# A two-layer encoder step: the modulation product moved into the input projections in four column groups, and the squares of the norms added up on VectorE

## The chip, the core and the metric

The kernel runs on one core of one Trainium2 chip. TensorE multiplies matrices (a product is a weight load, LDWEIGHTS, and a MATMUL that streams columns past the loaded weights), VectorE (DVE), ScalarE (ACT) and GpSimd (POOL) work element by element, and SyncE (SP) issues most DMAs. Each engine runs its own instructions in order and waits for others by semaphores. The metric is the device time of one execution in microseconds (us); lower is better.

## The reference, cut to what matters

A trunk of two layers is applied to 512 prompt tokens and 32 sample tokens, D = 1024, everything in float32.

```python
def trunk_layer(x, c, past, lw, layer):
    mod = einsum('bd,de->be', silu(c), lw['ada_w']) + lw['ada_b']     # 1024 -> 6144, per group
    sh1, sc1, g1, sh2, sc2, g2 = split(mod, 6)
    h = rms_norm(x, lw['norm_mix_g']) * (1 + sc1) + sh1
    z = h @ lw['w_in']                                # 2250 columns for the mixers, 3072 for the gates
    ...                                               # sparse, forgetting and pooling mixers
    x = x + g1 * (merged @ lw['w_out'])
    h = rms_norm(x, lw['norm_ffn_g']) * (1 + sc2) + sh2
    f = swiglu(h, ...) if layer % 2 == 0 else moe_ffn(h, ...)
    return x + g2 * f
```

`mod` is the modulation: for each of the two groups (prompt and sample) one row of 6144 values from the group's conditioning `c`, by a weight matrix of 1024 x 6144 (24 MB) per layer.

## The kernel before, in words

Activations lie transposed: `xT` and `hT` hold 8 blocks (k = 0 to 7) of 128 features by 544 tokens. A program order written out by hand runs on each engine; a planner class (`Ring`) works out, for four weight buffers `slots` of 1 MB, how often each has been filled (`full`) and which product must have begun before SP may fill it again (`free`). Per layer the stages are:

1. **First norm.** ACT squares the 8 blocks of x (L1299). TensorE sums them over the features with a matrix of ones, 8 blocks by 2 halves (`norm_sums`, L788). DVE takes mean and epsilon (L1570), ACT the root (L1304), DVE the reciprocal with one Newton step and the products `x * r` (`stats`, L1572 to L1577).
2. **Modulation** (L817 to L827). A loop of 6 rounds with 4 buffers each: TensorE multiplies silu(c) (`csil`, 128 x 2 per k) by 256 columns of the weights, 8 blocks of k, into 2 partitions; ACT copies the 2 x 256 row out (L1344), TensorE turns it into columns with two small products (L825). When all 24 blocks are through, DVE adds the bias (L1584) and forms the gains `scl` (L1587).
3. **norm** (ACT, L1316) applies gain and shift to each k, ACT rounds the result into a high part `hH` (L1323), DVE takes the rest as low part `hL` (L1592).
4. **z projection** (L843). 9 column blocks of 250, 5 token tiles each, so 45 tiles; a tile is 8 k by 3 products (high times high, high times low, low times high). ACT splits off the high part of each weight block (`proj_high`, L1336, into `wz`), POOL the low part (L674). ACT copies each tile out (L1352). DVE rotates queries and keys once 20 tiles are there (`rope`, L1607 to L1612).
5. Indexer scores (L870), gate projection (L882), selection, pooling, attention (L1002 to L1052), branch and output projections (L798, L882), residual sums on DVE (L1781).
6. **Second norm**: the same as stage 1 on the new x (`squares`, `norm_sums`, `stats`, `norm`).
7. Layer 0: a SwiGLU in two halves (L1235) written as loops on PE, ACT and DVE. Layer 1: a loop over expert passes (L1186, L1214).

What sets the order around the change: TensorE meets the modulation between the norm sums and the z projection, and the residual sums of the SwiGLU's last half come just before the first norm of layer 1. SP's queue holds the fills of one stage after those of the stage before. ACT calls the first `proj_high` of the gate projection while the last z block is multiplied.

```python
for k in range(KD):
    pe.wait_ge(sq_ready, KD * n + k + 1)
    for h in range(2):
        last = mm(ps[:, h, 0:HALF], ones[:, :], sqs[n % 2][:, k, h * HALF:(h + 1) * HALF], ...)
```

Of the kernel before, what the change touches and what calls it, by code (L numbers as in the profile page):

```python
# [52 lines left out]
MBLK, MSLOT = 20, 10  # L53
GU = 12
# [138 lines left out]
def encoder_step(nc, t_in, t_out):  # L193
    ring = Ring()
    for L in range(DEPTH):
        ring.phase(("ada", L), 6, [1] * 4)
        ring.phase(("z", L), ZITER, [1] * ZBODY)
        ring.phase(("gates", L), GITER, [1] * GBODY, slots=2)
        ring.phase(("pooled", L), 1, [1])
        ring.ghost()  # L200
        ring.phase(("branch", L), 2, [2] * 2)
        ring.phase(("out", L), 2, [1] * 2, slots=2)
        ring.ghost()

        if L == 0:
            ring.phase(("ffn", L), HALVES, [2] * FB + [1] * KD, "split")

    ctx = ExitStack()
    with ctx:
# [20 lines left out]
        def sem(name):  # L230
            return ctx.enter_context(nc.semaphore(name))
# [18 lines left out]
        csil = sb("csil", [P, KD, 2])  # L250
        mod = sb("mod", [P, 48, 2])
        scl = sb("scl", [P, 2, KD, 2])
        negcum = sb("negcum", [BH, KEYS])
# [74 lines left out]
        mrow = oTf[0:2, 4 * NTOK:4 * NTOK + 1024].rearrange("p (j n) -> p j n", j=4)  # L328
# [84 lines left out]
        ada_row, ada_copied, ada_done = sem("ada_row"), sem("ada_copied"), sem("ada_done")  # L413
# [7 lines left out]
        csil_ready = sem("csil_ready")  # L421
        mod_ready = sem("mod_ready")
        sq_ready, ms_ready, v_ready, root_ready = sem("sq_ready"), sem("ms_ready"), sem("v_ready"), sem("root_ready")
# [69 lines left out]

        def moe_landed(n, b):

            return n * 32 + 16 * (b // MSLOT + 1)
# [11 lines left out]
        def _(sp):  # L508
# [13 lines left out]
            for L in range(DEPTH):  # L522
                ada = t_in["ada_w"][L].rearrange("(k p) n -> p k n", p=P)
# [4 lines left out]
                def ada_fill(it):  # L528
                    for j in range(4):
                        fill(("ada", L), it, j, [(cols(j, 256), ada[:, :, ds(it * 1024 + j * 256, 256)])])  # L530

                if L == 0:
                    ada_fill(0)
                with sp.Fori(1 if L == 0 else 0, 6) as it:
                    if L == 0:
                        for j in range(4):
                            sp.wait_ge(block_begun, it * 4 + (j - 2))
                            sp.dma_start(cols(j, 256), ada[:, :, ds(it * 1024 + j * 256, 256)]).then_inc(slot_full[j], 16)
                    else:
                        ada_fill(it)  # L540
                with sp.Fori(0, ZITER) as it:
                    for j in range(ZBODY):
                        fill(("z", L), it, j, [(cols(j, ZB), w_in[:, :, ds(it * (ZBODY * ZB) + j * ZB, ZB)])])
# [99 lines left out]
        def _(pool):  # L643
# [14 lines left out]
            for L in range(DEPTH):  # L658
# [6 lines left out]
                pool.dma_start(poolm, t_in["c_pool"]).then_inc(pool_mats_loaded, 16)  # L665
# [13 lines left out]
                low(("gates", L), 0, 0)  # L679

# [75 lines left out]
        def _(pe):  # L756
# [26 lines left out]
            def norm_sums(n, releases=False):  # L783

                for k in range(KD):
                    pe.wait_ge(sq_ready, KD * n + k + 1)
                    for h in range(2):
                        last = mm(ps[:, h, 0:HALF], ones[:, :], sqs[n % 2][:, k, h * HALF:(h + 1) * HALF],  # L788
                                  start=(k == 0), stop=(k == KD - 1))
                        if releases and k == h == 0:  # L790
                            last.then_inc(block_begun, 1)
                last.then_inc(ms_ready, 1)
# [11 lines left out]
            for L in range(DEPTH):  # L804
# [6 lines left out]
                pe.wait_ge(v_ready, 2 * L + 1)  # L811
                with pe.Fori(0, 6) as it:
                    for j in range(4):
                        landed(("ada", L), it, j)
                        w = slots[:, j, :].rearrange("p (k n) -> p k n", k=KD)
                        for k in range(KD):
                            last = mm(ps[0:2, j, 0:256], csil[:, k, :], w[:, k, :], start=(k == 0), stop=(k == KD - 1))  # L817
                            if k == 0:
                                last.then_inc(block_begun, 1)
                        last.then_inc(ada_row, 1)  # L820
                        for i in ([j - 1] if j else []) + ([3] if j == 3 else []):

                            pe.wait_ge(ada_copied, it * 4 + (24 * L + i + 1))
                            for f in range(2):
                                last = mm(ps[:, 7, ds(it * 16 + (i * 4 + f * 2), 2)], mrow[:, i, f * P:(f + 1) * P],  # L825
                                          ident[0:2, 0:2], start=True, stop=True)
                            last.then_inc(ada_done, 1)  # L827

                with pe.Fori(0, ZITER) as it:
                    for j in range(ZBODY):  # L830
                        wh, wl, _ = proj_parts(("z", L), j)
                        for t in range(TILES):
                            g = j * TILES + t
                            if g >= TILES - 1:

                                pe.wait_ge(z_evac, it * (ZBODY * TILES) + (NZ * L + g - TILES + 2))
# [11 lines left out]
                    pe.wait_ge(z_evac, it * (ZBODY * TILES) + (NZ * L + ZBODY * TILES - 1))  # L848
# [257 lines left out]
                if L == 1:  # L1106
# [21 lines left out]

                    for s in range(2):
                        last = nc.tensor.transpose(ps[0:KD, 4, s * P:(s + 1) * P], mod[:, M_G2:M_G2 + KD, s], ident[:, :])  # L1130
# [149 lines left out]
        def _(act):  # L1280
# [10 lines left out]
            A(csil[:, :, :], vecT[:, 0, V_C:V_C + 16].rearrange("p (s k) -> p k s", s=2), ACT.Silu).then_inc(csil_ready, 1)  # L1291

            def squares(n, x_there):
                for k in range(KD):
# [32 lines left out]
            for L in range(DEPTH):  # L1327
                def proj_high(name, it, j):
# [4 lines left out]
                    act.wait_ge(block_begun, ring.released(name, it, j, ZBODY if name[0] == "z" else 2))  # L1333
# [4 lines left out]
                squares(2 * L, xu(L - 1, "ffn") - KD if L else None)  # L1338
                root(2 * L)

                with act.Fori(0, 6) as it:
                    for j in range(4):
                        act.wait_ge(ada_row, it * 4 + (24 * L + j + 1))
                        A(mrow[:, j, :], ps[0:2, j, 0:256], ACT.Copy).then_inc(ada_copied, 1)  # L1344
                norm(2 * L, lambda k, s: scl[:, 0, k, s:s + 1],
                     lambda k, s: mod[:, M_SH1 + k, s:s + 1], L + 1, split=True)

                def z_blocks(it):
                    for j in range(ZBODY):
                        for t in range(TILES):  # L1350
# [3 lines left out]
                            if t == 0:  # L1354

                                if j + 1 < ZBODY:
                                    proj_high(("z", L), it, j + 1)
                                elif isinstance(it, int):
                                    proj_high(("gates", L), 0, 0)
                                else:  # L1360
                                    proj_high(("z", L), it + 1, 0)

                with act.Fori(0, ZITER - 1) as it:
                    z_blocks(it)
                z_blocks(ZITER - 1)
# [80 lines left out]
                for j in range(2):  # L1446
                    proj_high(("out", L), 1, j)
                squares(2 * L + 1, xu(L, "start"))
                root(2 * L + 1)
                norm(2 * L + 1, lambda k, s: scl[:, 1, k, s:s + 1],  # L1450
                     lambda k, s: mod[:, M_SH2 + k, s:s + 1], 0)
# [66 lines left out]
                with act.Fori(0, HALVES) as it:  # L1518
# [22 lines left out]
                    for j in range(FB + KD):  # L1541
# [3 lines left out]
                        high(j, 1)  # L1545

        @block.vector
        def _(dve):
            ch = Chain(dve, dve_chain)
            V = nc.vector  # L1550
            V.memset(ones[:, :], 1.0).then_inc(memsets, 1)
# [26 lines left out]

            for L in range(DEPTH):
                stats(2 * L)  # L1580

                dve.wait_ge(ada_done, 24 * (L + 1))
                bias = vecT[:, L, V_ADAB:V_ADAB + 48].unsqueeze(2).to_broadcast([P, 48, 2])
                ch.link(V.tensor_tensor(mod[:, :, :], ps[:, 7, 0:96].rearrange("p (b s) -> p b s", s=2), bias, ALU.add))  # L1584
                for i, (sc0, g0) in enumerate(((M_SC1, V_NMIX), (M_SC2, V_NFFN))):
                    gain = vecT[:, L, g0:g0 + KD].unsqueeze(2).to_broadcast([P, KD, 2])
                    last = V.scalar_tensor_tensor(scl[:, i], mod[:, sc0:sc0 + KD, :], 1.0, gain, ALU.add, ALU.mult)  # L1587
                last.then_inc(mod_ready, 1)
# [26 lines left out]

                dve.wait_ge(z_evac, NZ * L + 4 * TILES)
                rope(IQ, IH)
                rope(IK, 1)
                rope(AQ, AH + 1)

# [322 lines left out]
                with dve.Fori(0, HALVES) as it:  # L1943
# [3 lines left out]
                    ch.enter(it, 0, 2 * FB)  # L1947

# [16 lines left out]
                    for j in range(FB + KD):  # L1965
# [5 lines left out]
                        if d >= 0:  # L1971
                            dve.wait_ge(unit_done[1], it * nb + (n0 * nb + FB + d + 1))
                            dve.wait_ge(x_upd, it * KD + (xu(L, "out") + d))
                            residual((d + 2) % 4, d, M_G2)
                    dve.wait_ge(unit_done[1], it * nb + (n0 * nb + FB + KD))
                    dve.wait_ge(x_upd, it * KD + (xu(L, "out") + KD - 1))
                    residual((KD + 1) % 4, KD - 1, M_G2)
                ch.leave(HALVES)
# [56 lines left out]
```

## Time and profile before

| what | us |
|---|---|
| median of 3 runs | 2545.38 |
| lowest, highest | 2542.48, 2548.31 |
| profiled execution, own time | 2540.93 |
| its span | 2539.1 |
| TensorE busy in the span | 2376.3 |
| DVE, ACT, POOL busy | 761.7, 579.2, 300.5 |

The span is the time from the first to the last instruction of one profiled execution. A row of the chain of waits gives start, length and what ran; the chain is followed back from the last instruction, each step to what released it. A row of the timeline names start, length, engine, line, operation, target and source tile, their shapes, how many were merged (x) and, in brackets, how long the engine had been idle and who released it. "PEclk" is the share of TensorE's full clock that was granted.

### The profile page before, as it was taken

What the parts mean: (1) busy time and instruction counts of PE and PEld (TensorE: products, weight loads), DVE (VectorE), ACT (ScalarE), POOL (GpSimd) and SP (SyncE); (2) the same over time, 40 slices, a digit from 0 to 9 for tenths busy, and PEclk for the clock granted to TensorE, in tenths of its full rate; (3) what the DMA queues carried; (4) which work ended last, traced back from release to release, by engine and by line L of the source; (5) the groups of instructions that cost most, each with busy time, mean ns of one, the idle gap of its engine ahead of it and who ended that gap; (6) DMA issues with size and microseconds to landing.
All of it is one profiled execution on the core that took longest, in us unless ns stands there. A gap on an engine that the chain in (4) does not pass through costs nothing.

```text
span 2539.1 us, 40187 instructions
## 1 busy us (share of the span) xinstructions
PE 2376.3 (94%) x16529; PEld 2115.6 (83%) x16531; DVE 761.7 (30%) x1561; ACT 579.2 (23%) x1158; POOL 300.5 (12%) x194
## 2 busy tenths in 40 slices
PE   6989899899959999999989899899989999999995
PEld 3479799776859999996479799666869999999995
DVE  2013490453433333332013580453430000000014
ACT  2042422131142222211042422231241111111111
POOL 2023343000210000000023332000210000000001
PEclk9989999896979999999989999896999999999998
DMA  6722222230243223225721232000266888777883
GB/s 223 240 82 65 85 83 83 66 106 15 77 120 83 64 81 100 84 65 175 237 69 55 86 99 67 13 1 25 79 213 202 247 261 267 247 231 232 244 283 114
DMA packets 333972, 328.04 MB, mean 129 GB/s; under 512 B 7659, under 2 KB 325593, under 8 KB 333305
## 3 DMA queue, kind: packets, MB, share of 16 engines
q1 hardware_dynamic: 326720, 303.41, 38.9%
q0 software_dynamic: 5888, 18.52, 2.2%
q10 hardware_dynamic: 1256, 4.60, 0.5%
q8 instruction: 78, 1.28, 0.2%
q14 instruction: 30, 0.24, 0.0%
HBM read 310.29 MB, written 26.16 MB: 133 GB/s over the span
## 4 chain that ended last, share of the span: by engine, by line
PE 92%; ACT 3%; DVE 2%; issue 1%; POOL 1%; DMA 1%; DVEq 0%; POOLq 0%; ACTq 0%; SPq 0%
PE ps L1235 16%; PE ps L882 16%; PE ps L1186 15%; PE ps L843 10%; PE ps L1214 7%; PE ps L817 7%; PE ps L798 5%; PE ps L1040 4%; PE ps L1024 3%; PE ps L1002 2%; PE ps L788 1%; PE ps L825 1%; ACT hT L1316 1%; PE ps L947 1%; PE ps L1163 1%
## 5 line engine op out<-in xcount | busy, mean ns | idle before, releaser
L1235 PE MATMUL ps<-hR,wR 128*128 128x272 f32 x2112 | 270.3, 291 | 31.2 <-DVE wR L1953 26.6
L882 PE MATMUL ps<-hH,slotsR 128*128 128x272 f32 x1536 | 293.7, 291 | 3.7 <-ACT oT L1385 3.7
L1235 PEld LDWEIGHTS ps<-hR,wR 128*128 128x128 f32 x2112 | 269.8, 191 | 31.8 <-DVE wR L1953 27.0
L882 PEld LDWEIGHTS ps<-hH,slotsR 128*128 128x128 f32 x1536 | 244.0, 190 | 4.4 <-issue 4.4
L674 POOL TENSOR_TENSOR slotsR<-slots,slotsR 128x1024 fp32r<-128x1024 f32 x64 | 154.5, 2435 | 699.2 <-ACT slotsR L1336 699.2
L843 PE MATMUL ps<-wz,hH 128*128 128x250 f32 (+1 forms) x720 | 206.7, 287 | 21.4 <-POOL slotsR L674 15.0
L882 PE MATMUL ps<-hL,slotsR 128*128 128x272 f32 x768 | 223.0, 290 | 0.0
L843 PE MATMUL ps<-slotsR,hH 128*128 128x250 f32 (+1 forms) x720 | 204.4, 284 | 0.0
L843 PE MATMUL ps<-wz,hL 128*128 128x250 f32 (+1 forms) x720 | 203.5, 283 | 0.0
L674 POOL TENSOR_TENSOR slotsR<-slots,wz 128x1000 fp32r<-128x1000 f32 x36 | 85.5, 2399 | 842.2 <-ACT wz L1336 842.2
L1186 PE MATMUL ps<-hg,slots 128*128 128x160 f32 x1280 | 177.3, 300 | 1.6 <-ACT hg L1476 0.6
L1186 PEld LDWEIGHTS ps<-hg,slots 128*128 128x128 f32 x1280 | 174.5, 190 | 3.6 <-issue 3.6
L817 PE MATMUL ps<-slots,csil 128*2 128x256 f32 x768 | 171.6, 379 | 2.4 <-DVE oT L1570 2.1
L1953 DVE TENSOR_TENSOR wR<-slots,wR 128x1024 fp32r<-128x1024 f32 (+1 forms) x76 | 82.3, 1085 | 262.2 <-ACT wR L1532 262.2
L843 PEld LDWEIGHTS ps<-wz,hH 128*128 128x128 f32 (+1 forms) x720 | 127.9, 178 | 25.3 <-POOL slotsR L674 15.1
L882 PEld LDWEIGHTS ps<-hL,slotsR 128*128 128x128 f32 x768 | 146.0, 190 | 0.0
L1532 ACT ACTIVATE wR<-slots 128x1024 fp32r<-128x1024 f32 (+1 forms) x76 | 71.9, 949 | 315.1 <-PE ps L1235 307.7
L817 PEld LDWEIGHTS ps<-slots,csil 128*2 128x2 f32 x768 | 62.2, 85 | 95.6 <-issue 3.1
L1186 PE MATMUL ps<-hg,w_more 128*128 128x160 f32 x1024 | 140.4, 299 | 0.0
L1186 PEld LDWEIGHTS ps<-hg,w_more 128*128 128x128 f32 x1024 | 139.5, 190 | 0.0
L1891 DVE TENSOR_TENSOR hidE<-ps,sgy 128x160 f32<-128x160 f32 x88 | 28.6, 325 | 364.2 <-PE ps L1186 355.2
L1235 PE MATMUL ps<-hidR,wR 128*128 128x272 f32 x1056 | 132.9, 288 | 0.0
(336 smaller groups left out, 3665.5 us busy)
## 6 DMA issues: line engine op xcount, KB each, us to landing
slots<-in_ada_w SPq DMA_DIRECT2D x48, 1024.0 KB, 5.2
slots<-in_w_in SPq DMA_DIRECT2D x24, 1024.0 KB, 5.2
slots<-in_w_in SPq DMA_DIRECT2D x18, 1000.0 KB, 5.0
slots<-in_moe_w_gate SPq DMA_DIRECT2D x16, 1024.0 KB, 6.2
slots<-in_moe_w_up SPq DMA_DIRECT2D x16, 1024.0 KB, 8.0
w_more<-in_moe_w_gate SPq DMA_DIRECT2D x16, 1024.0 KB, 5.5
w_more<-in_moe_w_up SPq DMA_DIRECT2D x16, 1024.0 KB, 8.0
w_more<-in_moe_w_down SPq DMA_DIRECT2D x16, 768.0 KB, 4.4
```

Source lines behind the costliest of these rows:

```text
L674: G.tensor_tensor(low_part[:, c], raw[:, c], high[:, c].bitcast(FP), ALU.subtract).then_inc(pw_split, 1)
L798: last = mm(ps[:, 2 * out_pair + h, 0:HALF], lhs(k), rhs(k)[:, h * HALF:(h + 1) * HALF], start=(k == 0), stop=(k == nk - 1))
L817: last = mm(ps[0:2, j, 0:256], csil[:, k, :], w[:, k, :], start=(k == 0), stop=(k == KD - 1))
L843: last = mm(ps[0:ROWS[t], t, 0:ZB], h[:, k, tok(t)], w[:, k * ZB:(k + 1) * ZB], start=(k == i == 0), stop=(k == KD - 1 and i == 2))
L882: last = mm(ps[:, 2 * out_pair + a, 0:HALF], w[:, c], r[:, n], start=(k == i == 0), stop=(k == KD - 1 and i == 2))
L1024: last = mm(ps[0:ROWS[t], 5 + tm % 2, h * HD:(h + 1) * HD], probsT[j % 2][0:kr, b * P:b * P + ROWS[t]], v, start=(b == 0), stop=final)
L1040: first = mm(out, qT[:, tok(t)], kT[:, KCOL[t]:KCOL[t] + w], start=True, stop=False)
L1186: last = mm(ps[:, 2 * w + f % 2, 0:CAP], wslot[b % MSLOT][:, k * width + c0:k * width + c0 + P], hg[:, k, :], start=(k == 0), stop=(k == K ...
L1214: last = mm(ps[:, 4 + d % 2, 0:CAP], wslot[b % MSLOT][:, c0:c0 + P], hidE[:, f, :], start=(f == 0), stop=(f == FB - 1))
L1235: last = mm(ps[:, 2 * out_pair + h, 0:HALF], wR[:, buf, a, k * P:(k + 1) * P], rhs(k, b)[:, c], start=(first and k == 0 and i == 0), stop= ...
L1532: A(wR[:, w, 0, 0:n], slots[:, j % NSLOT, c0:c0 + n], ACT.Copy).then_inc(w_high, 1)
L1953: V.tensor_tensor(wR[:, w, 1, 0:n], slots[:, j % NSLOT, c0:c0 + n], wR[:, w, 0, 0:n].bitcast(FP), ALU.subtract).then_inc(w_split, 1)
```

## The change: what it does

- The modulation stage is gone from the program between norm sums and projection. The 2 x 6144 row of each layer is worked out in 12 chunks of 512 columns, 24 for both layers. For a chunk the contraction's 8 blocks are dealt to four groups: group g multiplies blocks g and 4 + g into PSUM partitions 32g to 32g + 31 (`csil` is padded with zeros to 32 columns). ACT copies 128 x 512 out, TensorE transposes four 128 x 128 pieces, DVE adds the four groups with one reduction.
- The first 4 chunks (shift and gain of layer 0's first norm) run before the z projection of layer 0. Twelve more are placed after given tiles of layer 0's z projection (8 for layer 0, 4 for layer 1), the last 8 after tiles of layer 1's.
- Chunks get their weights in two fills of 1 MB; six places at first, three (`ada_x`, `ada_y`, slot 3) while z blocks hold slots 0 to 2. SP issues them in an order sorted with the z fills. The load of the pooling matrices waits until the chunks are through, since `ada_y` lies in their place. So does ACT's first `proj_high` of the gates, since slot 3 takes its result.
- The squares of a norm are added up on DVE as they come (`add_square`), and TensorE sums one block instead of eight. Squares of layer 1's first norm and of the second norms are taken as each residual sum is done.
- z loops on SP, PE and ACT and the SwiGLU loops on ACT and DVE are written out.

```diff
+AW = 512
+ADA_FIRST, ADA_LATER = 4, 8
+ADA_AT = [[1, 4, 8, 12, 16, 19, 23, 27, 31, 35, 39, 42], [6, 10, 14, 18, 23, 28, 34, 40]]
-        ring.phase(("ada", L), 6, [1] * 4)
+        ada_places = [0, 1, 2, 3, 4, 5, 3, 4] + [(5, 3, 4)[i % 3] for i in range(4 * ADA_LATER + 2 * ADA_FIRST)]
 # SP
+                    for u in range(2 * ADA_FIRST):
+                        ada_fill(u)
+                events = [(max(0, TILES * (b - 2)), 0, b) for b in range(ZITER * ZBODY)]
+                events += [(spots[(i - 3) // 2] + 1 if i >= 3 else 0, 1, i) for i in range(2 * len(spots))]
 # POOL
-                pool.dma_start(poolm, t_in["c_pool"]).then_inc(pool_mats_loaded, 16)
                 low(("gates", L), 0, 0)
+                pool.wait_ge(ada_used, 2 * (max(ada_hosted(L).values()) + 1))
+                pool.dma_start(poolm, t_in["c_pool"]).then_inc(pool_mats_loaded, 16)
 # PE
             def norm_sums(n, releases=False):
-                for k in range(KD):
-                    pe.wait_ge(sq_ready, KD * n + k + 1)
-                    for h in range(2):
-                        last = mm(ps[:, h, 0:HALF], ones[:, :], sqs[n % 2][:, k, h * HALF:(h + 1) * HALF], ...)
+                pe.wait_ge(sq_summed, n + 1)
+                for h in range(2):
+                    last = mm(ps[:, h, 0:HALF], ones[:, :], sqs[n % 2][:, 0, h * HALF:(h + 1) * HALF], start=True, stop=True)
+                def ada_rows(n, bank):
+                    if n:
+                        pe.wait_ge(ada_copied, n)
+                    for u in (2 * n, 2 * n + 1):
+                        pe.wait_ge(ada_full[ada_places[u]], ada_landed(u))
+                        for g in range(4):
+                            last = mm(ps[32 * g:32 * g + 32, bank, 0:AW], csil[:, (u % 2) * 4 + g, :],
+                                      ada_slots[ada_places[u]][:, g * AW:(g + 1) * AW], start=(u % 2 == 0), stop=(u % 2 == 1))
+                        last.then_inc(ada_used, 1)
+                def ada_columns(n):
+                    pe.wait_ge(ada_copied, n + 1)
+                    if n >= 2:
+                        pe.wait_ge(ada_summed, n - 1)
+                    for f in range(4):
+                        last = nc.tensor.transpose(ps[:, 6 + n % 2, f * P:(f + 1) * P], mrow[:, n % 2, f * P:(f + 1) * P], ident[:, :])
+                    last.then_inc(ada_done, 1)
                             last.then_inc(z_ready, 1)
+                            if at in hosted:
+                                ada_rows(hosted[at], 5)
+                            if at - 1 in hosted:
+                                ada_columns(hosted[at - 1])
 # ACT
+                            if at in hosted:
+                                ada_copy(hosted[at], 5)
+                act.wait_ge(ada_used, 2 * (max(hosted.values()) + 1))
+                proj_high(("gates", L), 0, 0)
+                        if it == HALVES - 1 and j > FB:
+                            squares(2, xu(1, "start") - KD, [j - FB - 1])
 # DVE
+            def add_square(n, k):
+                dve.wait_ge(sq_ready, KD * n + k + 1)
+                if k:
+                    total = sqs[n % 2][:, 0, :]
+                    last = V.tensor_tensor(total, total, sqs[n % 2][:, k, :], ALU.add)
+                def ada_sum(n):
+                    layer, c = ada_chunk(n)
+                    dve.wait_ge(ada_done, n + 1)
+                    V.tensor_reduce(mod[:, 4 * c:4 * c + 4, :], ps[:, 6 + n % 2, :].rearrange(...)[:, :, 0:2, :], AX.X, ALU.add)
                     residual(d % 4, d, M_G1)
+                    if d:
+                        add_square(2 * L + 1, d - 1)
+                add_square(2 * L + 1, KD - 1)
```

## Rows read from the trace of the kernel before

**Rows 1.** The page's chain that ended last, share of the span by line.
```profile
PE ps L1235 16%; PE ps L882 16%; PE ps L1186 15%; PE ps L843 10%; PE ps L1214 7%; PE ps L817 7%; PE ps L798 5%; PE ps L1040 4%; PE ps L1024 3%; PE ps L1002 2%; PE ps L788 1%; PE ps L825 1%; ACT hT L1316 1%; PE ps L947 1%; PE ps L1163 1%
```

**Rows 2.** Windows: length, busy us (count) by engine, PEclk, DMA share, GB/s.
```profile
36.00:134.00 98.00, 97.73 (x480) 43.27 (x478) 10.90 (x12) 9.15 (x25) 0.00 (x0) 1.00 0.73 233
170.00:276.00 106.00, 106.00 (x916) 104.84 (x915) 24.89 (x39) 27.55 (x53) 37.62 (x16) 1.00 0.19 59
284.30:286.20 1.90, 1.88 (x9) 1.37 (x10) 0.21 (x1) 0.62 (x2) 1.90 (x5) 0.50 1.00 365
```

**Rows 3.** Chain of waits in order of time: start us, length us, what.
```profile
52.32 7.07 PE ps L817 x32
...
68.73 7.07 PE ps L817 x32
...
151.23 125.24 PE ps L843 x1059
...
1271.45 1.13 ACT hT L1316 x2
...
1887.55 3.05 PE ps L1125 x24
```

**Rows 4.** Timeline of layer 0's start: squares, norm sums, statistics, modulation's end, norm.
```profile
20.83 0.60 ACT L1287 ACTIVATE xT<-ps 128x512 f32<-128x512 f32 x1 [0.26 <-PE ps L772]
...
26.41 4.46 ACT L1299 ACTIVATE z<-xT 128x544 f32<-128x544 f32 x8
...
27.19 7.57 PE L788 MATMUL ps<-z,ones 128*128 128x272 f32 x32 [1.73 <-ACT z L1299]
...
34.80 0.72 DVE L1570 TENSOR_SCALAR oT<-ps 128x544 f32<-128x544 f32 x1 [8.95 <-PE ps L788]
...
134.57 0.26 DVE L1587 SCALAR_TENSOR_TENSOR scl<-mod,vecT 128x16 f32<-128x16 f32 x2
134.87 1.12 ACT L1316 ACTIVATE hT<-hT,mod,scl 128x512 f32<-128x512 f32 x2 [1.36 <-DVE scl L1587]
```

**Rows 5.** Timeline of layer 0's second norm.
```profile
719.87 1.04 DVE L1781 SCALAR_TENSOR_TENSOR xT<-ps,mod,xT 128x272 f32<-128x272 f32 x3 [4.99 <-PE ps L882]
...
728.69 0.72 DVE L1570 TENSOR_SCALAR oT<-ps 128x544 f32<-128x544 f32 x1 [7.78 <-PE ps L788]
...
736.00 5.17 DVE L1577 TENSOR_TENSOR hT<-xT,oT 128x544 f32<-128x544 f32 x8
736.76 1.12 ACT L1316 ACTIVATE hT<-hT,mod,scl 128x512 f32<-128x512 f32 x2 [6.66 <-DVE hT L1577]
```

**Rows 6.** Timeline: the last residual sum of the SwiGLU.
```profile
1162.77 1.03 DVE L1781 SCALAR_TENSOR_TENSOR xT<-ps,mod,xT 128x272 f32<-128x272 f32 x3 [5.81 <-PE ps L1235]
```

**Rows 7.** Timeline of TensorE: indexer scores of 64 rows, heads alternating between partitions 0 and 64.
```profile
284.32 2.08 PE L870 MATMUL ps<-qk 64*128 64x256 f32 x8 [5.54 <-ACT qk L1378]
...
285.34 0.64 PE L870 MATMUL ps<-qk 64*128 64x256 f32 x2
...
286.19 1.10 PE L870 MATMUL ps<-qk 64*128 64x384 f32 x2
```

**Rows 8.** Timeline of TensorE: a product of 64 rows, then one of 128 rows.
```profile
519.69 0.59 PE L1040 MATMUL ps<-hT 64*128 64x512 f32 x1
520.21 0.33 PE L1002 MATMUL ps<-ident,pp 128*128 128x128 f32 x1
```

**Rows 9.** Groups of ACT: busy us, mean ns | idle us before, releasers.
```profile
L1336 ACT ACTIVATE slotsR<-slots 128x1024 fp32r<-128x1024 f32 x64 | 64.3, 1052 | 231.8 <-DMA slots<-in_w_out 139.8 <-DMA slots<-in_w_in 92.0
```

**Rows 10.** DMA issues of the page: count, KB each, median us from issue to landing.
```profile
slots<-in_ada_w SPq DMA_DIRECT2D x48, 1024.0 KB, 5.2
...
slots<-in_w_in SPq DMA_DIRECT2D x18, 1000.0 KB, 5.0
...
slots<-in_moe_w_up SPq DMA_DIRECT2D x16, 1024.0 KB, 8.0
```

**Rows 11.** Chain of waits after layer 0's z projection: ACT after the last tile.
```profile
276.87 1.28 ACT L1368
```

More of the change, by code:

```diff
@@ L327, in encoder_step @@
         oTf = oT[:, :, :].rearrange("p k n -> p (k n)")
-        mrow = oTf[0:2, 4 * NTOK:4 * NTOK + 1024].rearrange("p (j n) -> p j n", j=4)
+        mrow = oTf[:, 2816:2816 + 2 * AW].rearrange("p (j n) -> p j n", j=2)
+        place["gT_ada"] = (place["gT"][0] + ZBODY * KD * ZB * 4, SLOT * 4)
+        ada_x = sb("ada_x", [P, SLOT], over="gT_ada")
+        ada_y = pp[:, :, :, :].rearrange("p a b n -> p (a b n)")
+        ada_slots = [slots[:, i, :] for i in range(NSLOT)] + [ada_x[:, :], ada_y]
         score = oTf[:, 0:1312]
@@ L541, in _, with ada_fill @@
-                with sp.Fori(0, ZITER) as it:
-                    for j in range(ZBODY):
-                        fill(("z", L), it, j, [(cols(j, ZB), w_in[:, :, ds(it * (ZBODY * ZB) + j * ZB, ZB)])])
+                def ada_fill(u):
+                    layer, c = ada_chunk(u // 2)
+                    src = t_in["ada_w"][layer].rearrange("(k p) n -> p k n", p=P)
+                    if ada_places[u] in ada_places[:u]:
+                        before = max(i for i in range(u) if ada_places[i] == ada_places[u])
+                        sp.wait_ge(ada_used, before + 1)
+                    dst = ada_slots[ada_places[u]].rearrange("p (k n) -> p k n", k=4)
+                    sp.dma_start(dst, src[:, (u % 2) * 4:(u % 2) * 4 + 4, c * AW:(c + 1) * AW])\
+                        .then_inc(ada_full[ada_places[u]], 16)
@@ L810, in _ @@
                     pe.wait_ge(csil_ready, 1)
[L811 to L827, printed above, removed]
@@ L830, in _ @@
+                hosted = ada_hosted(L)
+                for it in range(ZITER):
                     for j in range(ZBODY):
@@ L1290, in _, with squares @@
             act.wait_ge(vt_evac, 1)
-            A(csil[:, :, :], vecT[:, 0, V_C:V_C + 16].rearrange("p (s k) -> p k s", s=2), ACT.Silu).then_inc(csil_ready, 1)
-            def squares(n, x_there):
-                for k in range(KD):
+            act.wait_ge(csil_clear, 1)
+            A(csil[:, :, 0:2], vecT[:, 0, V_C:V_C + 16].rearrange("p (s k) -> p k s", s=2), ACT.Silu).then_inc(csil_ready, 1)
+            def squares(n, x_there, which=range(KD)):
+                for k in which:
                     if x_there is not None:
@@ L1336, in proj_high, with ada_copy @@
                         A(high[:, c], raw[:, c], ACT.Copy).then_inc(pw_high, 1)
-                squares(2 * L, xu(L - 1, "ffn") - KD if L else None)
+                if L == 0:
+                    squares(0, None)
                 root(2 * L)
[L1341 to L1344, printed above, removed]
+                def ada_copy(n, bank):
+                    act.wait_ge(ada_used, 2 * n + 2)
+                    if n >= 2:
+                        act.wait_ge(ada_done, n - 1)
+                    A(mrow[:, n % 2, :], ps[:, bank, 0:AW], ACT.Copy).then_inc(ada_copied, 1)
+                if L == 0:
+                    for n in range(ADA_FIRST):
+                        ada_copy(n, 5)
                 norm(2 * L, lambda k, s: scl[:, 0, k, s:s + 1],
-                     lambda k, s: mod[:, M_SH1 + k, s:s + 1], L + 1, split=True)
-                def z_blocks(it):
+                     lambda k, s: mod[:, M_SH1 + k, s:s + 1], 2 * L + 1, split=True)
+                hosted = ada_hosted(L)
+                for it in range(ZITER):
                     for j in range(ZBODY):
@@ L1517, in _ @@
                 act.wait_ge(h_split, KD * (L + 1))
-                with act.Fori(0, HALVES) as it:
+                for it in range(HALVES):
                     n0 = fexp_base[L]
@@ L1545, in _ @@
                         high(j, 1)
+                        if it == HALVES - 1 and j > FB:
+                            squares(2, xu(1, "start") - KD, [j - FB - 1])
+                squares(2, xu(1, "start") - KD, [KD - 1])
         @block.vector
@@ L1579, in _ @@
+            for k in range(KD):
+                add_square(0, k)
             for L in range(DEPTH):
                 stats(2 * L)
[L1582 to L1587, printed above, removed]
@@ L1589, in _ @@
+                if L == 0:
+                    for n in range(ADA_FIRST):
+                        ada_sum(n)
+                    ada_finish(0, 0, 16, ADA_FIRST)
                 for k in range(KD):
@@ L1619, in _ @@
                 rope(AQ, AH + 1)
+                ada_hosted_sums([n for n in hosted if n not in early])
                 dve.wait_ge(z_evac, NZ * L + 8 * TILES)
@@ L1941, in _ @@
                     continue
-                with dve.Fori(0, HALVES) as it:
+                for it in range(HALVES):
                     n0 = fexp_base[L]
```

112 lines of the change are left out of this document (76 added, 36 removed).

## The prediction

> **What bounds the kernel now.** I read the chain of waits by line first: TensorE's lines fill it, and the modulation (L817, L825) holds 8% of the span, the norm sums (L788) 1% [rows 1]. The chain in order of time shows the pace: four blocks of 256 columns begin every 68.73 - 52.32 = 16.41 us, so six rounds are 98.5 us per layer, and nothing of the layer can run beside them [rows 3]. The windows say that in this stage TensorE is busy all the time at full clock, while the DMA engines move 233 GB/s; in the z projection TensorE is again busy all the time, and the DMA engines move only 59 GB/s [rows 2]. So the z stage has room for the weights, but none on TensorE: every product that is put there lengthens it. The timelines of the norms show the second bound: from the last residual sum to the first step of the statistics 7.78 us pass, most of it the 32 sum products, and some 8 us more until ACT can apply the norm [rows 5].
>
> All sums are made against the profiled execution's own 2540.9 us; the median of the runs shown lies 2545.4 - 2540.9 = 4.5 us above it, and I add that at the end.
>
> **Start of layer 0.** The squares end at 30.9 us (26.41 + 4.46) [rows 4]. Seven additions on DVE, at 5.17 / 8 = 0.65 us and about 0.1 us of handing over each [rows 5], trail them and end near 32.9; four sum products at 7.57 / 32 = 0.24 us and their drain give the statistics at 34.1 instead of 34.8. Then TensorE begins the four first chunks, which no longer wait for the statistics. A chunk uses one PSUM bank, so the next one waits for ACT's copy (0.60 us for 128 x 512 [rows 4]): 2.7 us per chunk with the rows' price below, so the first three have been multiplied by about 41. The fourth needs two fills that SP can send only when their places have been used, at 38.4 and 40.1; at 5.2 us to land [rows 10] they are there at 45.3, and with half a chunk, copy, transposes, reduction and two small DVE steps the gains are ready near 48.6. DVE itself could not be much earlier: its statistics take 8.07 us to the first product of x and r (728.69 to 736.76) and 4.4 more for the rest [rows 5], so to 46.7, and four reductions and the two steps follow. Before, the gains stood at 134.57 + 0.26 = 134.8 [rows 4]. Everything from there to the steady z stage stays as it is (16.4 us, to 151.2 [rows 3]). **Gain 86.2 us**, between 82 (fills that take 8.0 us as the slowest of [rows 10], or chunks at half clock) and 88.
>
> **First norm of layer 1.** The last residual sum ends at 1163.8 [rows 6]. Two additions of squares are left (blocks 6 and 7), 0.69 each with their waits; four sum products and drain 1.2: the statistics begin 2.6 us behind the residual sum, then the 8.07 us follow: ACT starts the norm at 1174.5. Before it started at 1271.45 [rows 3]. The statistics lay beside the modulation before and are now bare; that is in this sum. **Gain 97.0 us**, 95 to 98.
>
> **Second norms.** 2.6 us take the place of 7.78 [rows 5]: 5.2 us in each layer, **gain 10.4 us**. The extra additions on DVE and squares on ACT lie between residual sums that are about 5 us apart (4.99 and 5.81 of idle ahead of the last ones [rows 5, 6]), so I cost them at nothing; without that cover each block would add 0.7.
>
> **Price of a hosted chunk, on TensorE's path.** Its 8 float32 products are 16 instructions of 512 columns. One of 256 columns takes 7.07 / 32 = 0.221 us [rows 3], so 0.443 for 512. No row shows products in several column groups. The bounds: one after another, 16 x 0.443 = 7.1 us; all four groups side by side, 1.77. The nearest row is that of two row groups: in the indexer, heads alternate between partitions 0 and 64, and eight instructions of 256 columns go from 284.32 to 286.19, 0.234 each [rows 7], at a granted clock of 0.50 [rows 2], where one alone would take 2 x 0.221 = 0.44. Two groups thus give 1.89 times one, 95% of the ideal. I take the same 95% for four groups: 1.87 us. Changing the shape of the array costs little: 519.69 to 520.21 is 0.52 for 512 columns [rows 8], at most 0.08 over 0.443, twice per chunk: 0.18 with rounding up. Four transposes cost 4 x 3.05 / 24 = 0.51 [rows 3]. Sum 2.56 us. Twenty chunks (12 and 8) lie in z stages: **cost 51.2 us**. ACT's copies (0.60) and DVE's reductions fit in the idle time of these engines, which are busy 28 and 25 of 106 us there [rows 2]; DVE's rope holds back reductions for some 25 us, but the columns of a chunk wait only for the reduction two chunks earlier, so I cost that at nothing.
>
> The Trainium skill ("TensorE: Matmul & The Clock Gate", Part 3, measured speedup) has a number for column groups: three of them gave 2.38, which is 79% of the ideal. By that efficiency the rows of a chunk would take 2.24 us and the forecast would be 7 us later. No run here shows it yet.
>
> **What ACT does later.** The first high part of the gate projection, two copies of 1.05 us [rows 9], stood beside the last z block and now follows the last tile, where ACT's table loads and copies set the end [rows 11]. **Cost 2 x 2.1 = 4.2 us.** POOL's low part and the late load of the pooling matrices follow it and are wanted only by stages behind the indexer; the matrices' issue stands ahead of POOL's output DMAs, which nobody on the chain awaits.
>
> **Weights in time.** In layer 0's z stage some 27 fills of 1 MB (21 for chunks, 6 for z blocks) have to land in some 155 us, 182 GB/s, against 233 shown [rows 2]. A chunk's second fill is sent at least three tiles ahead, 3 x 125.2 / 45 = 8.3 us [rows 3], against 5.2 to land. I cost this at nothing, and between 0 and 15 us in the range. Loops written out: between a gain of 1 us and a loss of 5, taken as nothing, since the attention lines run written out with TensorE on the chain [rows 1].
>
> **Sum.** 2540.9 - 86.2 - 97.0 - 10.4 + 51.2 + 4.2 = 2402.7; with the 4.5 us of the runs **2407 us**, 5.4% faster. Own range 2393 to 2424.
>
> **Rivals.** (1) *Half the overlap.* Each float32 product is two instructions in the same group. If TensorE starts products strictly in program order, the second half of one group runs only beside the first half of the next, so two at a time: rows of 3.54 instead of 1.87 us, 20 x 1.67 = 33 us more, and 2 us at the start: **2442**. The timeline speaks against it: the heads of [rows 7] come in the same order of halves, yet two instructions stand in one row of 0.64 us, begun together, where a step of 0.44 between them would make it 1.07. This is what a rule of the Trainium skill would make of the case ("TensorE: Matmul & The Clock Gate", Part 3, what overlaps: products keep program order in start and end); the trace disagrees for row groups and has no column groups.
> (2) *No overlap: the change doesn't do what it says.* Rows 7.1 us: 20 x 5.2 = 104 us more, and the start ends near 67 instead of 48.6: 2407 + 104 + 18 = **2529**. For it: no column group is in the trace. Against: the row groups.
> (3) *Slower: late weights stop TensorE in the z stages.* TensorE takes its work in order, so a chunk whose fill is late stops the tiles behind it, and they are the path. To lose all that is gained, 2545 - 2407 = 138 us, each of 20 chunks must wait 6.9 us. A period is now 3.75 tiles and a chunk, 13 us, in layer 0, and three places mean that a fill must land within 1.5 periods; it decides from about 30 us between issue and landing on. **2550 and more.** For it: three times the traffic of the stage. Against: 5.0 to 8.0 us in [rows 10], also where 233 GB/s flow.
> (4) *The same, mild*: a few chunks with three tiles between them wait some us each, 2425 to 2440.
>
> **How the numbers follow.** Forecast 0.66, rival 1 0.15, rival 4 0.09, rival 2 0.06, rival 3 0.04. The range 2390 to 2460 takes in the forecast, rivals 1 and 4, and the bounds of the chunk's price. A difference under 0.2% (5 us) can't be told from none here; rival 2 lies 16 us below the old time, so nearly all cases but rival 3 are faster: faster 0.94, same 0.02, slower 0.04.
>
> **What would show it.** In the profile after: no stretch with modulation products alone but a short one near 34 to 47 us; gains of layer 0 near 49 us and the z products steady from 65; 16 instructions of 512 columns within about 1.9 us (3.5: rival 1, 7.1: rival 2); z stages of 125 + 31 and 125 + 20 us; waits of TensorE on the weights' DMA none (rival 3 or 4: some); ACT's norm in layer 1 about 10.7 us behind the last residual sum; 2.6 us from the last residual sum of a second norm to its statistics; 2 us more between the last z tile and the table loads. A z stage longer than 180 us in layer 0 would make the prediction wrong.

## The result, and the profile after

The changed kernel takes 2402.95 us (median of 4 runs, 2397.04 to 2403.8), the kernel before 2543.93 beside it: a ratio of 0.9447, interval 0.9431 to 0.9464, 5.5% faster. The forecast was 2407. The profiled execution took 2403.8 us, its span is 2401.9 against 2539.1.

The chain of waits of the changed kernel by line, the row that answers to [rows 1]:

```profile
PE ps L1283 17%; PE ps L929 16%; PE ps L1234 16%; PE ps L886 11%; PE ps L1262 8%; PE ps L831 5%; PE ps L1087 4%; PE ps L1071 3%; PE ps L1049 2%; PE ps L851 2%; ACT hT L1365 1%; PE ps L994 1%; PE ps L1211 1%; PE ps L1246 1%; DVE oT L1634 0%
```

The modulation's products are now L851 with 2%, where L817 and L825 had 8; the norm sums (L822, before L788) are no longer among the first lines. The windows of the two z stages (length, busy us of PE, PEld, DVE, ACT, POOL, granted clock, DMA share, GB/s) answer to the second of [rows 2]:

```profile
70.00:226.00 156.00, 155.30 (x1298) 134.89 (x1298) 28.47 (x56) 38.54 (x73) 38.86 (x16) 0.98 0.55 188
1138.00:1282.00 144.00, 143.83 (x1215) 129.87 (x1216) 24.84 (x50) 36.12 (x68) 37.47 (x16) 0.99 0.44 146
```

The stage's spare DMA time is used, 188 and 146 GB/s instead of 59, and TensorE still stands idle for less than 1 us in either. The chain in order of time (start us, length, what) at the start of layer 0, in its z stage, behind it, at its second norm and the start of its SwiGLU, and at layer 1's first and second norms, in place of [rows 3 to 6, 11]:

```profile
32.84 2.15 PE ps L822 x4
34.99 3.62 PE ps L851 x16
...
39.28 1.97 PE ps L851 x16
...
41.92 1.11 PE ps L851 x8
...
43.04 6.88 DMA ada_x<-in_ada_w
...
54.50 1.13 ACT hT L1365 x2
...
76.90 1.85 PE ps L851 x16
78.75 3.01 PE ps L886 x24
81.76 0.44 PE ps L861 x4
...
223.74 2.74 PE ps L886 x24
...
226.78 1.99 ACT slotsR L1387 x2
228.79 1.28 ACT L1426
...
671.69 1.04 DVE xT L1887 x3
...
674.39 2.16 PE ps L822 x4
...
684.78 1.13 ACT hT L1365 x2
...
701.64 201.10 PE ps L1283 x1584
...
1109.79 1.04 DVE xT L1887 x3
...
1112.48 1.17 PE ps L822 x4
...
1121.81 1.13 ACT hT L1365 x2
...
1724.06 1.04 DVE xT L1887 x3
...
1736.16 1.13 ACT hT L1365 x2
```

A hosted chunk, one that stands inside a z stage, can be read from it: 16 instructions in 1.85 us (76.90), later four transposes in 0.44 (81.76); the tile between them takes 3.01 us, where a tile takes 125.24 / 45 = 2.78 on average in the kernel before [rows 3]. ACT's norm of layer 0 starts at 54.50 instead of 134.87, that of layer 1 12.0 us behind the start of the last residual sum (1109.79) instead of 108.7 (1162.77 [rows 6] to 1271.45 [rows 3]). Not all of the early chunks keep that pace: the first takes 3.62 us, and the fourth waits for its second fill, sent at 43.04. A window over the first chunk (columns as above) shows a granted clock of 0.50:

```profile
34.99:38.60 3.61, 3.57 (x16) 0.52 (x16) 2.85 (x2) 0.66 (x1) 0.00 (x0) 0.50 0.00 0
```

Between landmarks of the two profiled executions, in us (a residual sum is counted from the start of its last row):

| step of the prediction | forecast | measured | from |
|---|---|---|---|
| start of layer 0, to the norm's first step | -86.2 | -80.4 | 134.87, now 54.50 |
| first norm of layer 1 | -97.0 | -96.7 | last residual sum to norm: 108.7, now 12.0 |
| second norms, both layers | -10.4 | -8.6 | last residual sum to norm: 16.9, now 13.1 and 12.1 |
| loops written out, ahead of the SwiGLU | 0 | -1.5 | norm's first step to the SwiGLU: 18.4, now 16.9 |
| 20 hosted chunks | +51.2 | +49.7 | norm's first step to the last z product: 141.3, now 171.7 and 160.6 |
| ACT's late gates part | +4.2 | +4.0 | last z product to indexer: 1.75 and 2.2 more |
| all the rest | 0 | -3.7 | the other stages |
| sum | -138.2 | -137.2 | spans 2539.1, 2401.9 |

The row for the loops is read from two starts of the SwiGLU, this one in the kernel before and 701.64 above:

```profile
751.69 1.09 issue
...
755.14 201.81 PE ps L1235 x1584
```

In the rest, layer 1 from the gate projection to the output projection is 4.3 us shorter on the same code (420.1 instead of 424.3). That is no gain of the change: the second profiled execution of the changed kernel has 425.5 there, and what differs most is the granted clock: in the output projection it is 1.00 (48.5 us), before it was 0.94 (51.0 us). The second set of runs of the changed kernel (below) has a median 3.8 us higher, so nothing under some 4 us is told from the runs alone. That the two sums agree to 1 us is therefore luck: the start and the second norms gave 7.6 us less than forecast, and the 4.3 us of layer 1 are most of what made up for it.

### The profile page after: what moved, and what is told of

Same layout as the page of the kernel before. It is cut to its first block, busy times and chain, and to the rows that moved or that the text cites. A ratio compares the mean times of both kernels' runs of the same rounds, so it can differ in the third digit from the quotient of the medians.

```text
span 2401.9 us, 38176 instructions
## 1 busy us (share of the span) xinstructions
PE 2215.7 (92%) x15939; PEld 2027.1 (84%) x15939; DVE 785.5 (33%) x1616; ACT 572.5 (24%) x1131; POOL 302.5 (13%) x194
## 4 chain that ended last, share of the span: by engine, by line
PE 90%; ACT 4%; DVE 3%; issue 1%; DMA 1%; POOL 1%; DVEq 0%; ACTq 0%; POOLq 0%; SPq 0%
PE ps L1283 17%; PE ps L929 16%; PE ps L1234 16%; PE ps L886 11%; PE ps L1262 8%; PE ps L831 5%; PE ps L1087 4%; PE ps L1071 3%; PE ps L1049 2%; PE ps L851 2%; ACT hT L1365 1%; PE ps L994 1%; PE ps L1211 1%; PE ps L1246 1%; DVE oT L1634 0%
## 5 line engine op out<-in xcount | busy, mean ns | idle before, releaser
L1283 PEld LDWEIGHTS ps<-hidR,wR 128*128 128x128 f32 x1056 | 132.7, 188 | 0.0
L886 PEld LDWEIGHTS ps<-slotsR,hH 128*128 128x128 f32 (+1 forms) x720 | 129.1, 179 | 0.9
```

The lines of the kernel that those rows point to most:

```text
L886: last = mm(ps[0:ROWS[t], t, 0:ZB], h[:, k, tok(t)], w[:, k * ZB:(k + 1) * ZB], start=(k == i == 0), stop=(k == KD - 1 and i == 2))
L1283: last = mm(ps[:, 2 * out_pair + h, 0:HALF], wR[:, buf, a, k * P:(k + 1) * P], rhs(k, b)[:, c], start=(first and k == 0 and i == 0), stop= ...
```

## The experiments

### How much of the gain is the side-by-side of column groups

Two kernels differ from the changed one only in the groups: all 8 products of a chunk in one, or alternating between two. ACT's copy, the transposes and DVE's step take only the partitions that are then used.

```diff
-  last = mm(ps[32 * g:32 * g + 32, bank, 0:AW], csil[:, (u % 2) * 4 + g, :], ...)
...
+  last = mm(ps[0:32, bank, 0:AW], csil[:, (u % 2) * 4 + g, :], ...)                            # one group
+  last = mm(ps[32 * (g % 2):32 * (g % 2) + 32, bank, 0:AW], csil[:, (u % 2) * 4 + g, :], ...)  # two groups
```

One group: 

> The changed kernel, but all eight products of a chunk go into one column group (partitions 0 to 31) and are added there; 32 rows are copied out and transposed, and no groups are left to add. Theory (the four groups run side by side and that is where a hosted chunk's low price comes from): the rows of a chunk take 16 x 0.43 = 6.9 us instead of 1.85, 20 chunks cost 100 us more, and the start of layer 0 gets about 15 us longer: 2515 to 2525 us. Rival (the gain comes from putting the products beside the z work and its weights' loads, and the groups matter little): rows within 1.85 to 3 us, 2403 to 2425 us.

Two groups: 

> The changed kernel with two column groups of four products each. Theory (time of a chunk's rows goes as one over the number of groups, whole groups run side by side): rows of 3.7 us, 20 x 1.85 = 37 us more and some 3 us at the start: 2438 to 2446 us. Rival (two halves of a float32 product must follow each other in program order, so overlap comes in another proportion): two groups would give rows of 4.3 us or more (5 steps where the theory has 4), 2450 us or more.

Measured: 2521.26 us (ratio to before 0.9926, 0.9904 to 0.9947) and 2441.6 (0.9619, 0.9595 to 0.9642). The chains of one group, and then of two, have these rows for a chunk:

```profile
105.95 6.99 PE ps L851 x16
```

```profile
106.94 3.56 PE ps L851 x16
```

So the 16 instructions take 6.99, 3.56 and 1.85 us in one, two and four groups: two are 1.96 and four 3.78 times as fast as one. Without the groups the change would have been worth 20 us instead of 140.

### Squares summed on TensorE again

```diff
-  pe.wait_ge(sq_summed, n + 1)
-  for h in range(2):
-      last = mm(ps[:, h, 0:HALF], ones[:, :], sqs[n % 2][:, 0, ...], start=True, stop=True)
+  for k in range(KD):
+      pe.wait_ge(sq_ready, KD * n + k + 1)
+      for h in range(2):
+          last = mm(ps[:, h, 0:HALF], ones[:, :], sqs[n % 2][:, k, ...], start=(k == 0), stop=(k == KD - 1))
```

DVE's additions are left out with it. 

> The changed kernel with the squares summed by 32 products on TensorE again, DVE's additions taken out. Theory (the 32 products after the last residual sum are what the DVE additions saved): 4 to 5 us more at each of the three norms behind a residual sum, about 1 us at the start: 2415 to 2419 us. Rival (the squares being taken early by ACT is what saved the time, the additions only replace one wait by another): 2401 to 2406 us.

Measured: 2414.48 us (2412.04 to 2415.35; ratio 0.9508, 0.9488 to 0.9528), 8 to 12 us over the two medians of the changed kernel and 0.5 under the expected range. Its chain, at the start of layer 0 and at the second norm there:

```profile
34.30 1.90 PE ps L853 x16
...
40.64 6.63 DMA ada_x<-in_ada_w
...
51.85 1.13 ACT hT L1367 x2
...
665.83 1.04 DVE xT L1882 x3
666.91 7.62 PE ps L823 x32
...
682.75 1.13 ACT hT L1367 x2
```

The second norm has its 7.62 us of sum products back, and the norm starts 16.9 us behind the start of the residual sum (665.83 to 682.75) instead of 13.1. The three norms behind a residual sum lose 3.8, 4.8 and 4.8 us. At the start of layer 0 it is the other way round: the chunks begin 0.7 us earlier and at full clock (1.90 instead of 3.62), so the fourth chunk's second fill is sent at 40.64 instead of 43.04, and the norm starts at 51.85 instead of 54.50. There the additions on DVE cost 2.6 us; the forecast had a gain of 0.7.

### Is hosting needed, or would fast chunks do

All 12 chunks of layer 0 run ahead of its z projection, as a stage of their own in six places:

```diff
-ADA_FIRST, ADA_LATER = 4, 8
+ADA_FIRST, ADA_LATER = 12, 0
+ADA_AT = [[8, 18, 28, 38], ...]
...
-  ada_places = [0, 1, 2, 3, 4, 5, 3, 4] + [(5, 3, 4)[i % 3] ...]
+  ada_places = [i % 6 for i in range(2 * ADA_FIRST)] + [(3, 4, 5)[i % 3] for i in range(24)]
```

> The changed kernel with all 12 chunks of layer 0 ahead of its z projection as a stage of their own, in four column groups, with six places for the weights; the 12 of layer 1 are hosted as before (4 in layer 0, 8 in layer 1). Theory (alone, a chunk waits for its 2 MB, so hosting and groups need each other): 8 more chunks at the start need 16 MB at about 300 GB/s, 56 us, and 8 hosted chunks less give back 20 us: 2430 to 2445 us, with TensorE waiting on the weights' DMA in the first 110 us. Rival (only TensorE's own time counts, wherever it stands): 2400 to 2408 us.

Measured: 2420.86 us (2420.63 to 2423.45; ratio 0.9535, 0.9515 to 0.9556). The direction was expected, the size was not: the loss is 14 to 18 us, not 27 and more. The chain, and a window over the stage:

```profile
45.59 13.46 DMA slots<-in_ada_w
59.04 14.34 DMA pp<-in_ada_w
...
91.83 1.12 ACT hT L1365 x2
```

```profile
36.00:100.00 64.00, 37.84 (x242) 11.69 (x234) 16.23 (x31) 15.45 (x27) 3.66 (x2) 0.87 1.01 365
```

From 45.59 on the stage waits for weights: the DMA engines are full at 365 GB/s (a busy share of 1.01), above the rate that I had put in, and TensorE is busy in 38 of 64 us. The norm starts 37.3 us later than in the changed kernel, and 8 hosted chunks of 2.5 us fall away. Fast chunks outside the projections are bound by the transfer; inside them it is covered.

### Two waits that the change itself brought in

*Early fills*: the fourth chunk's fills get places of their own (6 and 7, in the tile that the z projection will fill later). *Gates early*: ACT's first high part goes back beside the last z block, and the hosted chunks end earlier for it. *Both* has both edits.

```diff
-  ada_places = [0, 1, 2, 3, 4, 5, 3, 4] + [(5, 3, 4)[i % 3] ...]
+  ada_places = [0, 1, 2, 3, 4, 5, 6, 7] + [(3, 4, 5)[i % 3] ...]
...
```

```diff
-ADA_AT = [[1, 4, 8, 12, 16, 19, 23, 27, 31, 35, 39, 42], [6, 10, 14, 18, 23, 28, 34, 40]]
+ADA_AT = [[1, 4, 7, 11, 14, 18, 21, 24, 28, 31, 35, 39], [6, 10, 14, 18, 22, 27, 33, 38]]
...
+                            if at == ZITER * ZBODY * TILES - 4:
+                                act.wait_ge(ada_used, 2 * (max(hosted.values()) + 1))
+                                proj_high(("gates", L), 0, 0)
-                act.wait_ge(ada_used, 2 * (max(hosted.values()) + 1))
-                proj_high(("gates", L), 0, 0)
```

Early fills: 

> The two fills of the fourth chunk get places of their own, so they need not wait until the first chunks have been multiplied. Theory (the fourth chunk's weights are the last thing that the start of layer 0 waits for): they land near 41 to 43 us instead of 49.97, the wait of 1.93 us goes, and the fourth chunk follows the third directly; the first ACT step of the norm comes at 49 to 51 us instead of 54.5, the time is 2397 to 2400 us. Rival (the slow half clock of TensorE and DVE's own chain bound the start): the wait goes, but the norm's first step stays within 1 us of 54.5, and the time stays at 2402 to 2404 us.

Gates early: 

> The first high part of the gate projection stands beside the last z block again, and the hosted chunks end three tiles earlier, with as little as three tiles between two of them. Theory (ACT's two copies of 1 us are bare on the path behind the last tile, in both layers): the gap between the last z product and the gates' products falls by 1.7 us in layer 0 and 2.2 in layer 1, the time is 2398 to 2400 us. Rival (the chunks that stand closer together wait for their weights, or the table loads set the gap): TensorE waits on weights in the z stages, some 1 to 5 us in all, and the time is 2402 us or more.

Both: 

> Both edits, places of their own for the fourth chunk's fills and the gates' high part beside the last z block. If the two theories hold they lie in different stages and add up: 2393 to 2396 us. If one of them fails: 2398 to 2400. If both fail: 2402 to 2404.

The changed kernel again: 

> The changed kernel as it is, on the chip of the three others, so that differences of 4 us can be told: 2403 us, within 2 us.

Measured: early fills 2399.14 us (ratio 0.9438, 0.9422 to 0.9454), gates early 2399.52 (0.9454, 0.9438 to 0.947), both 2395.19 (0.9428, 0.9414 to 0.9441), the changed kernel again 2406.76 (0.9464, 0.9448 to 0.948), which is 3.8 us above its first set and a miss of the 2 us that I had given it. The single edits lie within each other's intervals, so the traces have to decide. The chain of early fills, start of layer 0:

```profile
42.68 5.17 DVE hT L1643 x8
47.85 0.21 DVE mod L1666 x2
...
48.10 1.08 PE ps L865 x8
...
49.86 1.13 ACT hT L1369 x2
```

The wait for the fill is gone, the norm starts at 49.86 instead of 54.50, and what is last now is DVE's own chain: statistics, products of x and r, reductions. The chain of gates early behind layer 0's z projection:

```profile
225.78 0.37 ACT z L1411
226.17 1.28 ACT L1427
```

No copy of 1 us stands before the table loads any more. TensorE's wait there (us in total over both layers, times, longest), in the changed kernel and then in gates early:

```profile
PE ps L917 <- ACT qk L1436: 14.9, 2, 7.4
```

```profile
PE ps L917 <- ACT qk L1437: 11.1, 2, 5.5
```

It falls to what it was before the change, 11.1 us, and TensorE waits for the modulation's weights nowhere but at the start of layer 0, three tiles between chunks notwithstanding. Both theories hold, 4.6 and 3.8 us in the traces. Together they lie 7.8 and 11.6 us under the two medians of the changed kernel (the interval is clear of that of its second set, and overlaps the first's by 0.001): a version that beats the kernel before and, by runs and trace, the changed one.

### How far the weights are from being late

Rival 3 is tried by taking places away from the hosted fills: two instead of three, and one.

```diff
-  ada_places = [0, 1, 2, 3, 4, 5, 3, 4] + [(5, 3, 4)[i % 3] ...]
+  ada_places = [0, 1, 2, 3, 4, 5, 3, 4] + [(3, 4)[i % 2] ...]      # two
+  ada_places = [0, 1, 2, 3, 4, 5, 3, 4] + [3] * (4 * ADA_LATER + 2 * ADA_FIRST)   # one
```

Two: 

> The hosted chunks' weights get two places instead of three, so both fills of a chunk can be sent only when the same half of the chunk before has been used. Theory (a fill lands in 5 to 8 us, and the next chunk is at least three tiles, 8.3 us, away): TensorE still waits on no weights in the z stages, 2403 to 2407 us. Rival (the weights are just in time, and the third place is what hides them): waits of 1 to 5 us at the chunks, 2420 us or more.

One: 

> One place only: a chunk's second fill can be sent only when TensorE has used the first, in the middle of the chunk, so its landing is bare. Theory: each of the 20 hosted chunks waits about a landing, 4 to 5.2 us, and nothing else changes: 2403 + 80 to 104 = 2483 to 2507 us. It is the price of late weights, a known one. If the fills that SP holds back also delay the z blocks' weights: more than 2510 us. If landings are hidden in another way: under 2450.

Measured: 2408.5 us with two (2404.26 to 2409.69; ratio 0.9472, 0.9457 to 0.9488), which is 1.5 over the expected range and not to be told from the changed kernel's second set, and 2556.76 with one (2550.46 to 2557.09, and one run at 2620.55; without that run the ratio is 1.0045, 1.0029 to 1.0061). The waits of TensorE by line and releaser (us in total, times, longest), with two places and then with one:

```profile
PE ps L851 <- DMA ada_x<-in_ada_w: 2.7, 1, 2.7
...
PE ps L851 <- DMA slots<-in_ada_w: 2.3, 1, 2.3
```

```profile
PE ps L851 <- DMA slots<-in_ada_w: 105.0, 21, 5.3
```

With two places both waits are the old ones of layer 0's start (2.5 and 2.0 us in the changed kernel), so the third place is margin. With one, 20 hosted chunks wait 5.2 us each, as expected, 103 us in all, and that is not the whole: the z stages are 148 us longer. The explanation that I had ready for more than 2510 us, late z weights, is not it: the z products wait for nothing new. The chain and the windows of the kernel with one place show the rest:

```profile
76.97 1.04 PE ps L851 x8
...
78.02 4.99 DMA slots<-in_ada_w
...
83.06 1.94 PE ps L851 x8
85.00 3.68 PE ps L886 x24
```

```profile
83.06:85.00 1.94, 1.94 (x9) 0.28 (x9) 0.00 (x0) 0.00 (x0) 0.00 (x0) 0.50 0.00 0
70.00:315.00 245.00, 182.70 (x1299) 147.68 (x1299) 24.31 (x56) 39.22 (x73) 37.69 (x16) 0.83 0.39 128
1227.00:1432.00 205.00, 163.19 (x1225) 139.07 (x1226) 22.71 (x50) 37.45 (x70) 37.13 (x16) 0.88 0.34 113
```

Behind the wait of 5 us TensorE runs at a granted clock of 0.50: the second half of the chunk takes 1.94 us, and the next 24 z products 3.68 instead of 3.01. The second halves of all twenty chunks take 1.83 to 1.94 us, the first halves 1.07. About as many instructions as in the changed kernel's windows keep TensorE busy 27.4 us longer in layer 0 (182.70 - 155.30) and 19.4 in layer 1. So a late fill costs 5.2 us of waiting and some 2.3 of half clock (46.8 / 20), and twenty of them undo the whole gain: rival 3 is a real mechanism with a real price, two places away.

## Why the prediction was right, and where its terms were off

**The chunk's price**, the step with the widest bounds (7.1 to 1.77 us), was 1.85 us against 1.87 for the rows, and 2.5 against 2.56 in all (0.44 of it transposes, some 0.2 in the tile behind). The reading of [rows 7] carried it: two row groups side by side at 95% of the ideal, and four column groups at 3.78 of 4, also 95%. The kernels with two groups and one have the row times that rivals 1 and 2 gave to four: 3.56 and 6.99 us (forecast 3.54 and 7.1), and nearly their times, 2441.6 and 2521.26 us (forecast 2442 and 2529). The Trainium skill ("TensorE: Matmul & The Clock Gate", Part 3, measured speedup) has 2.38 for three column groups, 79% of the ideal; no run here has three, and the row of 1.85 us shows 95% for four. A rule of the Trainium skill in the same part (what overlaps: products keep program order in start and end) was named beside rival 1 and its 3.54 us in four groups; the trace has 1.85, so what rival 1 made of it does not hold here. The rows name no column group, so whether single instructions keep that order is not shown.

**The start of layer 0** was the term that was most off, 80.4 us instead of 86.2 and below its own lower bound of 82. The forecast had "chunks at half clock" or slow fills at that end and took full clock and 5.2 us as its values; something of both came. The trace has the sums at 2.15 us for four products and the first chunk at 3.62, granted clock 0.50 behind 7.66 us in which TensorE had nothing to do: DVE's additions, which replaced 7.57 us of products [rows 4], had taken its work away. The kernel with sums on TensorE shows that by itself: first chunk 1.90 us. The fourth chunk's second fill landed at 49.93, not 45.3: it was sent at 43.04, not 40.1, and took 6.88 us instead of 5.2, with three z fills sent right behind it. Early fills gives back 4.6 us of the 5.8. Its chain stands at 49.86, where the prediction had put the whole start at 48.6, with DVE's chain just below, at 46.7 and the reductions behind it.

**First norm of layer 1** (96.7 against 97.0) came as worked out: DVE takes one addition behind ACT's last square, four products take 1.17 us, and the statistics stand bare behind them. **Second norms** gave 8.6 of 10.4: 3.8 in layer 0 and 4.8 in layer 1, where 5.2 each was forecast. In layer 0 the four products ran at a granted clock of 0.50 and took 2.16 us, so the statistics began 3.9 us behind the residual sum and not 2.6; in layer 1 they began 2.9 us behind it. That the earlier additions hide between residual sums holds in these three places. In the kernel with sums on TensorE the three norms lose 13.4 us, and the early start takes 2.6 of that back.

**ACT's late gates part**, 4.0 against 4.2, is confirmed by its undoing, 3.8.

**Weights in time** held, with a margin that the prediction had no row for: no wait in the z stages with two places, 5.2 us per chunk and the half clock with one. The landing itself was taken too short, 5.2 us: in the changed kernel the modulation's fills take 7.5 us in the median into the slots, 7.1 and 6.0 into the two other places, and the z blocks' 6.6 instead of 5.0. The places covered it:

```profile
slots<-in_ada_w SPq DMA_DIRECT2D x18, 1024.0 KB, 7.5
```

Rival 3 had been given its deciding point at 6.9 us per chunk; with one place the waits alone are 5.2 and the half clock makes up the rest, 7.4 (148 / 20), so the time lands above the old one, which 5.2 alone would not have done.

**Loops written out** were costed at nothing; layer 0's SwiGLU begins 1.5 us sooner behind its norm and is 0.5 us longer, no more than an execution's own scatter. No kernel was run with these loops alone, so their share is not shown.

**The 4.5 us** added for the runs did not recur: the changed kernel's profiled execution took 2403.8 us and its median is 2402.95, so set against that execution the forecast is 2402.7.

## What to carry to other kernels

A product with few output rows leaves much of the array unused, here 6.99 us in one column group where four groups take 1.85: deal its contraction to column groups and add them up afterwards, and its cost is divided by nearly their number, here 3.78 of 4. Then put it where the stream of weights is covered: the same chunks as a stage of their own are bound by their DMA, and inside a stage that TensorE fills they cost only their own 2.5 us, as long as every fill has a place ahead. Price a late fill by its wait and by what TensorE's clock does behind it, and be wary of emptying TensorE just ahead of a stage that it must do fast. When a sum of terms comes out right, compare the terms: here two were off by 7.6 us, and the scatter of one execution hid it.

## What the runs showed that was not expected

- A wait of 5 us in a busy stage costs 7.4 us: behind it TensorE's products run at half clock (granted 0.50, 1.94 us for eight instructions, where 16 take 1.85 at full clock).
- Moving 28 of 32 sum products off TensorE made the following chunk slower, 3.62 instead of 1.90 us, at the one place where TensorE had nothing else to do before, for 7.66 us. In front of the three later norms it has nothing to do for 2.8 us: in the ten profiled executions with sums on DVE the four products behind that took 1.15 to 1.26 us in 23 cases and 2.15 in 7. What decides between the two the runs do not show.
- One core's load of weights alone ran at 365 GB/s over 64 us, with the DMA engines full; the modulation stage of the kernel before had moved 233 with TensorE as its bound [rows 2].
